# Two MLPs in one decoder kernel: up projections as seven block products for eight over pairs of tiles, with squares kept in DRAM until a separate down phase

## What is computed

```
h = modulate(rmsnorm(x, g), sh2, sc2)
y = square(relu(h @ mlp_w_up[layer])) @ mlp_w_down[layer]     # 1024 -> 4096 -> 1024
x = x + g2 * y
```

## Time and profile before

| what | us |
|---|---|
| three runs | 2724.46, 2727.78 (median), 2729.19 |
| the profiled execution | 2731.49 |
| its span | 2729.7 |
| TensorE busy in the span | 2647.9 |
| vector, scalar, GpSimd busy | 1219.2, 777.5, 149.3 |
| first MLP, about | 645 to 1348 |
| second MLP, about | 2024 to 2727 |

### The profile page before, as it was taken

The page is one execution under the profiler, slowest core; times in us unless marked ns, Lnnn a source line. Parts: engine busy times, 40 slices in busy tenths (PEclk is TensorE's granted clock), DMA queues, the critical chain, the costliest instruction groups (busy, mean ns, idle before and its releaser), DMA issues.

```text
span 2729.7 us, 34859 instructions
## 1 busy us (share of the span) xinstructions
PE 2647.9 (97%) x14016; PEld 2223.5 (81%) x14016; DVE 1219.2 (45%) x1366; ACT 777.5 (28%) x1173; POOL 149.3 (5%) x152
## 2 busy tenths in 40 slices
PE   6999999999999999999999997999999999999999
PEld 4999998778888888888899886666688888888887
DVE  5436434447444444443533543777254333333332
ACT  5436222113211122112211333777233112211120
POOL 0000000000000000000000002666000000000000
PEclk9999999999999999999989997999999999999999
DMA  6331422221323332321222353554211111111111
GB/s 271 101 109 39 163 92 82 88 81 51 101 93 102 99 93 92 105 79 53 107 68 82 108 166 104 129 128 111 110 39 55 47 54 47 46 46 46 54 47 70
DMA packets 77026, 242.69 MB, mean 89 GB/s; under 512 B 7936, under 2 KB 24320, under 8 KB 73728
## 3 DMA queue, kind: packets, MB, share of 16 engines
q1 hardware_dynamic: 76928, 241.29, 27.8%
HBM read 211.90 MB, written 29.36 MB: 88 GB/s over the span
## 4 chain that ended last, share of the span: by engine, by line
PE 90%; DVE 5%; ACT 2%; DMA 1%; issue 1%; POOL 1%; SPq 0%; ACTq 0%; DVEq 0%; POOLq 0%
PE PS L1506 22%; PE PS L1508 22%; PE PS L1507 22%; PE PS L1608 5%; PE PS L1609 5%; PE PS L1610 5%; DVE KEEP L1427 2%; PE PS L1850 1%; PE PS L1863 1%; PE PS L1831 1%; ACT PS L911 1%; PE PS L1787 1%; PE PS L1832 1%; POOL A L605 1%; DVE H_LO L1030 1%
## 5 line engine op out<-in xcount | busy, mean ns | idle before, releaser
L1506 PE MATMUL PS<-H_HI,W_HI 128*128 128x512 f32 x1280 | 501.8, 392 | 3.1 <-DVE H_LO L1030 3.1
L1508 PE MATMUL PS<-H_HI,W_LO 128*128 128x512 f32 x1280 | 498.4, 389 | 0.0
L1507 PE MATMUL PS<-H_LO,W_HI 128*128 128x512 f32 x1280 | 498.1, 389 | 0.0
L1192 DVE SCALAR_TENSOR_TENSOR X<-PS,MODV,X 128x1024 f32<-128x1024 f32 x148 | 189.9, 1283 | 471.3 <-PE PS L1508 471.3
L1506 PE MATMUL PS<-HID_HI,W_HI 128*128 128x512 f32 x1024 | 398.9, 390 | 0.0
L1508 PE MATMUL PS<-HID_HI,W_LO 128*128 128x512 f32 x1024 | 398.4, 389 | 0.0
L1507 PE MATMUL PS<-HID_LO,W_HI 128*128 128x512 f32 x1024 | 398.4, 389 | 0.0
L356 ACT ACTIVATE W_HI<-RAW 128x1024 fp32r<-128x1024 f32 x208 | 216.4, 1052 | 620.0 <-PE PS L1508 551.4
L1608 PE MATMUL PS<-W_HI,H_HI 128*128 128x256 f32 x1216 | 349.1, 287 | 5.9 <-DVE H_LO L1030 5.7
L1610 PE MATMUL PS<-W_LO,H_HI 128*128 128x256 f32 x1216 | 347.0, 285 | 0.0
L1609 PE MATMUL PS<-W_HI,H_LO 128*128 128x256 f32 x1216 | 347.0, 285 | 0.0
(11 more groups left out here) (144 smaller groups left out, 2988.0 us busy)
## 6 DMA issues: line engine op xcount, KB each, us to landing
RAW<-in_wt SPq DMA_DIRECT2D x208, 512.0 KB, 3.5
MODRAW<-in_modw SPq DMA_DIRECT2D x96, 512.0 KB, 4.5
QK<-qk_scratch SPq DMA_DIRECT2D x16, 768.0 KB, 6.3
MOD<-in_modw SPq DMA_DIRECT2D x8, 1024.0 KB, 18.2
qk_scratch<-KOUTA SPq DMA_DIRECT2D x16, 512.0 KB, 5.8
qk_scratch<-KOUTB SPq DMA_DIRECT2D x16, 512.0 KB, 3.8
QK<-qk_scratch SPq DMA_DIRECT2D x16, 512.0 KB, 8.1
X<-in_xT SPq DMA_DIRECT2D x4, 1024.0 KB, 8.0
```

The costliest lines, as they stand in the source:

```text
L1192: dve.scalar_tensor_tensor(X[:, k, :], flat(acc(u % 2)), MODV[:, gate + k:gate + k + 1], X[:, k, :], ALU.mult, ALU.add).then_inc(sem["acc_ ...
L1506: pe.matmul(dst, w_hi, m_hi, start=first, stop=False)
L1507: pe.matmul(dst, w_hi, m_lo, start=False, stop=False)
L1508: return pe.matmul(dst, w_lo, m_hi, start=False, stop=last)
```

## The change

In each MLP the first four up tiles stay as four quarter units. Their results are copied out by the scalar engine, relu-squared in SBUF by one vector instruction (`plain`), and stored to DRAM (`hid_scratch`, HIDD). The other 28 up tiles are taken in 14 pairs. A pair is a 2 x 2 block product (two output tiles; two halves of the depth of 1024; two halves of the tokens), made from seven block products instead of eight, in the Strassen-Winograd form. Sums of weight blocks S1 to S4 (GpSimd, four of 128x512 a pair) and sums of activation blocks T1 to T4 (GpSimd and vector, once an MLP) are cut into HI and LO like the rest. Each product is 4 blocks of depth x 3 terms = 12 matmuls into one of banks 0 to 5; the seventh goes to bank 2 again. Scalar copies product 1 to SBUF (`keep`), vector builds the four results from seven sums (`combine`), relu-squares each (`finish`), and each is stored (256 KB). After the last pair the down phase reads the squares back, 2 MB for a group of four tiles, cuts them (HRAW to HID_HI and HID_LO), and runs all 32 down tiles with the gate added into X as before. X is spilled to DRAM (4 MB) at the start, since the pairs' weights lie in its place, and comes back in two halves during the last pair. The conditioning work is spread over both phases (three in two pairs, then one a down tile).

The core of the diff:

```diff
+UPS = FF // P
+PAIRS = UPS // 2 - 2
+PRODUCTS = 7
+BLOCKS = 6
+A1, S2, S1, S3, S4, A22 = range(BLOCKS)
...
+        BLOCK_AT = {A1: (0, 0), S2: (1, 0), S1: (1, 1), S3: (2, 0), S4: (2, 1), A22: (3, 0)}
...
+        PRODUCT_BANK = [0, 1, 2, 3, 4, 5, 2]
+        MLPS = ((1, 1, T_M0, U_M0), (4, 3, T_M1, U_M1))
...
+            def mlp(m, mods):
+                r, s, t0, u0 = MLPS[m]
+                sp.wait_ge(sem["acc_free"], freed(u0 - 1))
+                sp.dma_start(XD[:], X[:]).then_inc(sem["x_spilled"], 16)
...
+                def store(p, order, f, c, half):
+                    tile = (p * 2 + 4 + f).v
+                    if order is not None:
+                        sp.wait_ge(sem["h_made"], count_of(m, p, 4, order + 1).v)
+                    sp.dma_start(HIDD[tile, :, half_of(half)], HS[p % 2][:, c, :]
+                                 ).then_inc(sem[f"hs_out{p % 2}"], 16)
+
+                def load_pair(p):
+                    sp.wait_ge(sem["w_lo"], blocks_cut(m, p, A22).v)
+                    for f in range(2):
+                        sp.dma_start(RAW[:, f, :], wt[(p * 2 + t0 + 6 + f).v]).then_inc(sem[f"raw_in{f}"], 16)
+
+                def two_pairs(i, stop=2):
+                    for x in range(stop):
+                        p = Count(x, 2, i) if i is not None else Count(2 * (PAIRS // 2 - 1) + x)
+                        load_pair(p)
+                        store(p, 0, 0, 0, 0)
+                        if mods:
+                            load_mod(sp, p // 2 * 3 + 49 + 2 * x)
+                        if mods and x == 0:
+                            load_mod(sp, p // 2 * 3 + 50)
+                        store(p, 2, 0, 1, 1)
+                        store(p, 3, 1, 2, 0)
+                        store(p, None, 1, 3, 1)
...
+                load_pair(p)
+                sp.wait_ge(sem["product"], count_of(m, p, PRODUCTS, 1).v)
+                for b in range(2):
+                    sp.wait_ge(sem[f"hs_out{b}"], 16 * UPS * m + 64)
+                sp.dma_start(HRAWX[:], HIDD[0:4].rearrange("j p s -> p j s")).then_inc(sem["hr_in0"], 16)
+                sp.dma_start(X[:, 0:4, :], XD[:, 0:4, :]).then_inc(sem["xm_lo"], 16)
+                store(p, 0, 0, 0, 0)
+                if mods:
+                    load_mod(sp, Count(69))
+                load_raw(sp, Count(t0 + UPS + 2))
+                sp.wait_ge(sem["hid_lo"], UPS * m + 4)
+                sp.dma_start(X[:, 4:8, :], XD[:, 4:8, :]).then_inc(sem["xm_hi"], 16)
+                store(p, 2, 0, 1, 1)
+                load_raw(sp, Count(t0 + UPS + 3))
+                store(p, 3, 1, 2, 0)
+                store(p, None, 1, 3, 1)
+                load_raw(sp, Count(t0 + UPS + 4))
...
+                for b in range(2):
+                    sp.wait_ge(sem[f"hs_out{b}"], 16 * UPS * (m + 1))
+
+                def load_hid(g, e):
+                    sp.dma_start(HRAW[e][:], HIDD[bass.ds((g * 4).v, 4)].rearrange("j p s -> p j s")
+                                 ).then_inc(sem[f"hr_in{e}"], 16)
+
+                load_hid(Count(1), 1)
...
+                    pool.tensor_tensor(lo[S1], raw_block(1, 0), raw_block(1, 1), ALU.add).then_inc(sem["w_sum"], 1)
+                    pool.wait_ge(sem["w_sum"], (done + 1).v)
+                    pool.tensor_tensor(lo[S2], lo[S1], raw_block(0, 0), ALU.subtract).then_inc(sem["w_sum"], 1)
+                    pool.wait_ge(sem["w_sum"], (done + 2).v)
+                    pool.tensor_tensor(lo[S4], raw_block(0, 1), lo[S2], ALU.subtract).then_inc(sem["w_sum"], 1)
+                    pool.tensor_tensor(lo[S3], raw_block(0, 0), raw_block(1, 0), ALU.subtract).then_inc(sem["w_sum"], 1)
...
+                pool.wait_ge(sem["h_lo"], 16 * r + 12)
+                t_sum(1, *h_exact(0, 0), ALU.add)
+                t_sum(3, *h_exact(0, 1), ALU.add)
+                pool.wait_ge(sem["t_sum"], 6 * m + 2)
+                t_sum(1, t_raw(3), t_raw(1), ALU.subtract)
+                pool.wait_ge(sem["h_lo"], 16 * r + 16)
+                t_sum(2, *h_exact(1, 1), ALU.add)
+                pool.wait_ge(sem["t_sum"], 6 * m + 4)
+                t_sum(3, t_raw(2), t_raw(3), ALU.subtract)
+                pool.wait_ge(sem["t_sum"], 6 * m + 5)
+                t_sum(2, t_raw(2), t_raw(1), ALU.subtract)
+                pool.wait_ge(sem["x_spilled"], 16 + 32 * m)
+                weight_sums(Count(0), 0)
...
+                    pool.wait_ge(sem["product"], count_of(m, p, PRODUCTS, 1).v)
+                    weight_sums(p + 1, (p + 1) % 2)
...
+                def keep(p, x):
+                    act.wait_ge(sem["product"], count_of(m, p, PRODUCTS, 1).v)
+                    act.activation(HS[x][:, 0, :], PS[:, PRODUCT_BANK[0], :], ACT.Copy).then_inc(sem["s_kept"], 1)
...
+                def combine(p, x, n, after, bank, a, c):
+                    dve.wait_ge(sem["product"], count_of(m, p, PRODUCTS, after).v)
+                    if n == 1:
+                        dve.wait_ge(sem["s_kept"], count_of(m, p, 1, 1).v)
+                    else:
+                        dve.wait_ge(sem["c_made"], count_of(m, p, PRODUCTS, n - 1).v)
+                    dve.tensor_tensor(HS[x][:, c, :], PS[:, bank, :], HS[x][:, a, :], ALU.add).then_inc(sem["c_made"], 1)
+
+                def finish(p, x, n, c):
+                    h = HS[x][:, c, :]
+                    dve.wait_ge(sem["c_made"], count_of(m, p, PRODUCTS, n).v)
+                    dve.scalar_tensor_tensor(h, h, 0.0, h, ALU.max, ALU.mult).then_inc(sem["h_made"], 1)
+
+                def c11(p, x):
+                    combine(p, x, 1, 3, PRODUCT_BANK[2], 0, 1)
+                    combine(p, x, 2, 3, PRODUCT_BANK[1], 0, 0)
+                    finish(p, x, 2, 0)
+
+                def c22(p, x):
+                    combine(p, x, 3, 5, PRODUCT_BANK[4], 1, 2)
+                    combine(p, x, 4, 5, PRODUCT_BANK[3], 1, 1)
+                    combine(p, x, 5, 5, PRODUCT_BANK[3], 2, 3)
+                    finish(p, x, 5, 3)
+
+                def c12(p, x):
+                    combine(p, x, 6, 6, PRODUCT_BANK[5], 1, 1)
+                    finish(p, x, 6, 1)
+
+                def c21(p, x):
+                    combine(p, x, 7, 7, PRODUCT_BANK[6], 2, 2)
+                    finish(p, x, 7, 2)
...
+                def pair(p, x, first=False, last=False):
+                    if first:
+                        t4_sum()
+                    if last:
+                        c11(p, x)
+                        if mods:
+                            mod_reduce(dve, p // 2 * 3 + 50)
+                        cut_lo(dve, Count(t0 + UPS))
+                        hid_lo(Count(0), 0, 0, HRAWX)
+                        cut_lo(dve, Count(t0 + UPS + 1))
+                        c22(p, x)
+                        for j in range(1, 4):
+                            hid_lo(Count(0), j, 0, HRAWX)
+                        c12(p, x)
+                        cut_lo(dve, Count(t0 + UPS + 2))
+                        c21(p, x)
+                        return
+                    block_cut(p + 1, 1 - x, A1)
+                    c11(p, x)
+                    if mods:
+                        mod_reduce(dve, p // 2 * 3 + 48 + 2 * x)
+                    block_cut(p + 1, 1 - x, S2)
+                    block_cut(p + 1, 1 - x, S1)
+                    if first:
+                        t_cut(4)
+                    block_cut(p + 1, 1 - x, S3)
+                    c22(p, x)
+                    if mods and x == 0:
+                        mod_reduce(dve, p // 2 * 3 + 49)
+                    block_cut(p + 1, 1 - x, S4)
+                    block_cut(p + 1, 1 - x, A22)
+                    c12(p, x)
+                    c21(p, x)
...
+                    if following:
+                        if j == 0:
+                            for b in range(2):
+                                dve.wait_ge(sem[f"hs_out{b}"], 16 * UPS * m + 16 * UPS)
+                        hid_lo(g + 1, j, 1 - e, HRAW[1 - e])
...
+                def product(n, w, h):
+                    for k in range(4):
+                        mm = three(PS[:, PRODUCT_BANK[n], :], w[0][:, k, :], w[1][:, k, :], h[0][:, k, :], h[1][:, k, :],
+                                   k == 0, k == 3)
+                    mm.then_inc(sem["product"], 1)
...
+                    block_in(A1)
+                    if first:
+                        pe.wait_ge(sem["acc_free"], freed(u0 + 2))
+                    else:
+                        pe.wait_ge(sem["s_kept"], count_of(m, p, 1, 0).v)
+                    product(0, block_pair(x, 0, 0), h_block(0, 0))
+                    made(-5)
+                    product(1, block_pair(x, 0, 1), h_block(1, 0))
+                    block_in(S2)
+                    t_in(2)
+                    if first:
+                        pe.wait_ge(sem["acc_free"], freed(u0 + 3))
+                    made(0)
+                    product(2, block(S2), t_block(2))
+                    block_in(S1)
```

(17 more changed lines are left out.)

467 lines of the change are left out of this document (321 added, 146 removed).

## The result

The changed kernel takes 2831.45 us (median; 2830.22 to 2833.5), the kernel before 2726.97 beside it. The ratio is 1.0384 with a 95% interval of 1.0366 to 1.0402: 104.5 us slower. The sign was forecast, the size wasn't: the time lies 83 us above the forecast and 37 above the upper end of its range.

The account below looks back on a forecast made before the run. TensorE, busy for 97% of the span, was taken as the bound. 2731.5 - 76.1 - 3.1 + 21.8 + 21 + 39.4 + 17.4 = 2751.9, as a median 2748 us against 2727.8 (0.7% slower); range 2704 to 2794.

Parts of the forecast that it names:

- hand-over: From the pairs to the down phase: TensorE waits 12.3 us for the last sum, 7.4 for X, per MLP; +39.4 us.
- matmuls that go: In 28 pairs, 84 matmuls instead of 96, each worth 0.2265 us: -76.1 us.
- waits for H_LO go: In the quarter units that begin each MLP, TensorE's waits for H_LO may vanish: -3.1 us.
- start of the pair phase: Sums of activations and cuts before the first product delay TensorE, both MLPs: +21.8 us; bounds 0 and 35.
- pair loop: The 14 pairs of each MLP run slower than TensorE's 19.03 us a pair: +21 us; bounds 0 and 64.
- clock: Half clock after each of six waits over 5 us, 2.9 us lost each: +17.4 us (0 to 20).
- Bound and saving: TensorE bounds the kernel: a matmul removed saves 0.2265 us, a new wait costs its length; 76.1 us of matmuls saved.
- the second chain: At the hand-over, from C21 through X's upper half, stores and group 1 of squares to the first add: 43.9 us.
- the ring: Pair loop: loads, cuts, sums and C21, whose stores precede the next loads; 20.35 us first MLP, 19.75 second.
- The rival for this: GpSimd holds vector's relu-square and a cut: ring 1.3 us longer, +40 in all, 2788 us; chance 0.18.
- The rival with the right mechanism: Vector and GpSimd get in each other's way on instructions with two SBUF operands: +40, 2788 us; chance 0.18.
- Transfers that overlap: Rival: queues serve transfers side by side, shortening pair ring and hand-over: 2707 us; chance 0.25.

Follow-up runs that it names:

- unread sums: Changed kernel, cuts not waiting for GpSimd's four weight sums a pair: 2755.47 us with the sums left out, 2827.24 us with GpSimd making four that nobody reads.

## Why the prediction was wrong

The terms of the sum against the profile of the changed kernel, in us. The measured waits are those of the list above less those of the kernel before; of the waits for HS, two count as hand-over: 9.5 us, which end at 1039.81, and 10.1 in the second MLP.

| Step | predicted | measured |
|---|---|---|
| matmuls that go | -76.1 | -76.1 (336) |
| waits for H_LO go | -3.1 | +9.8 |
| start of the pair phase | +21.8 | +38.2 (34.2 and 4.0 of issue) |
| pair loop | +21 | +44.8 (64.4 - 9.5 - 10.1), waits alone |
| hand-over | +39.4 | +34.6 (19.6 and 15.0 for X) |
| clock | +17.4 | +50.8 (the remainder) |
| sum | +20.4 | +102.1 |

- **Bound and saving: right**, as far as the account shows: with each matmul at its 0.2265 us and each wait at its length it closes with a remainder that the clock can hold, and the steady down phase cost nothing.
- **Hand-over: right**, chain and size. C21 of the last pair but one ends at 1014.39 in the first MLP and the last sum of the phase, which starts at 1039.07, at 1039.75: 25.4 us, where I had put 25.6. The waits were 9.5 and 10.1 for 12.3, and 9.1 and 5.9 for 7.4. That their sum fits so well is partly luck: in the first MLP TensorE came to its wait 15.9 us after C21, not 13.3, and the second chain took 47.4 us for 43.9.
- **Pair loop: the ring was right, its length wasn't, and this is the main failed step.** Every cut and relu-square beside GpSimd went into the ring at its undisturbed row. The ring lasts 22.19 us in the first MLP and 21.86 in the second, where I had 20.35 and 19.75; without the sums it is 20.01 in the first and no longer the bound in the second. So contention is 2.15 us a pair in the first MLP. The rival for this had 1.3, one relu-square and one cut; it is one relu-square and three cuts. The price is more than the waits in the table: over 19.03 us a pair, the eleven periods come to 34.8 us in the first MLP and 31.1 in the second, 66 in all, where I had 21 for all pairs. TensorE waits in only 39 of these 66; in the rest it does its matmuls at the lower clock, within a length that the ring sets.
- **Start: three steps failed.** GpSimd's 2048 columns were scaled from attention's rows to 3.6 us; they take 4.64 with the vector engine idle (9.28 for two, from 691.05) and 5.03 on average for the sums of H_HI and H_LO, which run beside vector instructions, so the six sums that start at 669.66 (I had 670.0) end at 700.3, not at 691.8. And the sums don't run beside the cuts of H but in turns with them: the waits for H_LO, which I let go, grew to 12.9 us, and the vector engine's three cuts of T took 9.81 us for 6.8. Last, block A1 was cut in 5.52 us for 1.14, beside GpSimd's part of T4. The block was ready at 717.9, not at 701.0, and TensorE stood there from 700.3, not from 691.6: 17.7 us for 9.4. The Trainium skill (GPSIMD Engine Reference, 3.1) gives 4497 ns for such an add, 3% under the 4.64 us measured. The sum went by the row of another instruction instead.
- **Clock: the step that failed is the count of waits.** I charged 2.9 us for each of six waits over 5 us and nothing for the short ones. The pairs, whose longest wait between 740 and 1010 is 3.6 us and in the second MLP 3.1, ran at 0.95 and 0.94 all the same, the start at 0.88 and the hand-over at 0.77. Between 740 and 1010 the clock fell to 0.50 at five of the seven waits (those of 3.4 to 3.6 us) and 3.1 us were lost each time; in the second MLP it did so at waits of 1.8 to 3.1 us and didn't at others of 2.3. What divides these no run here shows. Some 24 of the 50.8 us are in the pairs, where, as I read it, they only fill time that the ring would have left idle, so about 27 stand against the 17.4 of the sum. The lost share times the length of the six windows of start, pairs and hand-over in both MLPs comes to 60 us at most, idle time included, which bears the remainder of 50.8 out.
- **Two bounds were too narrow by the sum's own rules.** GpSimd at twice its row would have made each start 21.6 us longer, 65 us in all and not 35, and 2 us more in the ring gives 21 + 28 x 2 = 77, not 64.
- **The rival with the right mechanism** had a chance of 0.18 and a price of 40 us. What spoke against it, GpSimd's constant rows in attention, was no evidence, as the text itself had said: the vector engine reads PSUM there. The pair of runs with and without unread sums shows 72 us for the weight sums alone, clock included, and the H block sums are worth up to 22 more. Transfers that overlap were not seen: from the end of C21 (881.09) to the scalar engine's cut of the first load (886.33) there are 5.2 us, where I had 4.85, and the first group of squares was used 12.5 us after C21, where I had 12.4.

## What to carry to other kernels

Before work is moved to GpSimd, list the vector instructions that will run beside it and mark those with two operands in SBUF. Each may have to wait for the whole of GpSimd's instruction, so a long GpSimd instruction is only free while the vector engine idles or has an operand in PSUM. A ring that closes through a DMA queue within a microsecond of TensorE's time deserves to be opened before it is tuned: issuing the next loads ahead of three stores was worth 66 us here and made the contention in the pairs nearly harmless. A new wait on a TensorE that never waited costs its length and, as the waits of 3.6 us and less showed, can cost clock as well. Where a ring sets the pace, price (period minus TensorE's work) times rounds; the lower clock is then part of it and not a cost beside it.
